# Six stores of a start value issued ahead of the first gather, in a mixer and mixture-of-experts block

## The reference, cut to what matters

```python
logits = (h @ router_w + router_b).astype(jnp.float32)
top_v, top_i = lax.top_k(logits, TOP_K)
gates = jax.nn.softmax(top_v, axis=-1).astype(h.dtype)
...
def expert_block(args):
    xblk, e = args
    gu = xblk @ w_gu[e] + b_gu[e]
    gate = jnp.minimum(gu[:, ::2], SWIGLU_LIMIT)
    up = jnp.clip(gu[:, 1::2], -SWIGLU_LIMIT, SWIGLU_LIMIT)
    act = (up + 1.0) * gate * jax.nn.sigmoid(SWIGLU_ALPHA * gate)
    return act @ w_down[e] + b_down[e]

yb = lax.map(expert_block, (xb, block_e))
y = yb.reshape(-1, D)[dest] * gate_sorted[:, None]
return jnp.zeros_like(h).at[tok_sorted].add(y)
```

## Time and profile before

| | |
|---|---|
| median of 3 runs | 2887.31 us (2883.24 to 2889.01) |
| profiled execution, its own time | 2882.61 us |
| its span in the trace | 2880.8 us |
| PE busy | 2584.2 us, 90% |
| DVE busy | 1755.5 us, 61% |
| ACT busy | 1550.8 us, 54% |
| POOL busy | 761.7 us, 26% |
| moved by q1 (SP and others) | 481.80 MB |
| moved by q0 (POOL) | 47.79 MB |

### The profile page before, as it was taken

The page is one execution under the profiler, slowest core; times in us unless marked ns, Lnnn a source line. Parts: engine busy times, 40 slices in busy tenths (PEclk is TensorE's granted clock), DMA queues, the critical chain, the costliest instruction groups (busy, mean ns, idle before and its releaser), DMA issues. The chain is left out here.

```text
span 2880.8 us, 132861 instructions
## 1 busy us (share of the span) xinstructions
PE 2584.2 (90%) x55873; PEld 2238.8 (78%) x55873; DVE 1755.5 (61%) x1936; ACT 1550.8 (54%) x1833; POOL 761.7 (26%) x586
## 2 busy tenths in 40 slices
PE   8999997898898886699999999998889999999993
PEld 2444556788888754598998998988888999999993
DVE  2344894544545477517264638577787767878883
ACT  3522543433333543517264647577777767768773
POOL 1201003543544212112222222232222322233221
PEclk9999998999999997799999999999999999999997
DMA  9500001000000222818365659698899887979975
GB/s 366 192 30 32 1 1 37 19 26 15 18 25 15 84 96 104 341 24 285 119 209 192 227 173 342 219 329 319 316 351 308 307 291 272 326 276 350 348 276 194
DMA packets 124477, 536.74 MB, mean 186 GB/s; under 512 B 12541, under 2 KB 13553, under 8 KB 91617
## 3 DMA queue, kind: packets, MB, share of 16 engines
q1 hardware_dynamic: 107120, 481.80, 44.6%
q0 software_dynamic: 14464, 47.79, 7.3%
q10 hardware_dynamic: 2832, 6.37, 0.6%
HBM read 496.99 MB, written 38.92 MB: 186 GB/s over the span
## 5 line engine op out<-in xcount | busy, mean ns | idle before, releaser
L2192 PE MATMUL ps<-qkv,weights 128*128 128x64 f16 x10496 | 939.7, 193 | 71.7 <-DVE weights L1686 37.4
L2192 PEld LDWEIGHTS ps<-qkv,weights 128*128 128x128 f16 x10496 | 922.2, 98 | 87.6 <-DVE weights L1686 43.9
L2193 PE MATMUL ps<-qkv,weights 128*128 128x64 f16 x10496 | 939.1, 193 | 2.3 <-issue 2.3
L2194 PE MATMUL ps<-qkv,weights 128*128 128x64 f16 x10496 | 939.1, 193 | 0.0
L2193 PEld LDWEIGHTS ps<-qkv,weights 128*128 128x128 f16 x10496 | 922.9, 98 | 2.4 <-issue 2.4
L2194 PEld LDWEIGHTS ps<-qkv,weights 128*128 128x128 f16 x10496 | 922.9, 98 | 0.0
L1686 DVE SCALAR_TENSOR_TENSOR weights<-hT,weights 128x2048 f16<-128x2048 f32 x256 | 592.5, 2373 | 170.3 <-ACT weights L1147 145.2
L1147 ACT ACTIVATE weights<-hT 128x2048 f16<-128x2048 f32 x256 | 523.2, 2098 | 75.1 <-DMA hT<-in_w_gu_dram 66.2
L2209 PE MATMUL ps<-qkv,weights 128*128 128x64 f16 x5248 | 472.0, 193 | 20.8 <-DVE weights L1691 18.6
L2209 PEld LDWEIGHTS ps<-qkv,weights 128*128 128x128 f16 x5248 | 461.4, 98 | 27.4 <-DVE weights L1691 23.0
L2210 PE MATMUL ps<-qkv,weights 128*128 128x64 f16 x5248 | 471.7, 193 | 0.0
(11 more groups left out here) (395 smaller groups left out, 3979.8 us busy)
## 6 DMA issues: line engine op xcount, KB each, us to landing
hT<-in_w_gu_dram SPq DMA_DIRECT2D x256, 1024.0 KB, 6.9
qkv<-in_w_down_dram SPq DMA_DIRECT2D x128, 1024.0 KB, 5.7
weights<-in_w_ada_dram SPq DMA_DIRECT2D x12, 2048.0 KB, 16.4
qkv<-in_w_in_dram SPq DMA_DIRECT2D x4, 2048.0 KB, 7.7
hT<-decay_rows SPq DMA_DIRECT2D x20, 256.0 KB, 3.3
hT<-beta_rows SPq DMA_DIRECT2D x20, 256.0 KB, 3.9
qkv<-in_x_dram ACTq DMA_DIRECT2D x8, 512.0 KB, 6.6
weights<-in_w_in_dram SPq DMA_DIRECT2D x2, 2048.0 KB, 14.5
```

What stands on the lines that cost most here:

```text
L2192: pe.matmul(dst, ghi[k][:, b, c], xT[:, 0, k, :], start=first, stop=False, skip_group_check=True)
L2193: pe.matmul(dst, ghi[k][:, b, c], xT[:, 1, k, :], start=False, stop=False, skip_group_check=True)
L2194: last = pe.matmul(dst, glo[k][:, b, c], xT[:, 0, k, :], start=False, stop=end, skip_group_check=True)
```

## The change

POOL issues the stores of pieces 0 to 5 ahead of `gather(0)`, and those of pieces 6 and 7 behind it. Nothing is added or taken away; the same transfers are issued by the same engine on the same queue in another order. Pieces 6 and 7 stay behind, since PE makes them only after it has turned the gathered rows.

```diff
             pool.sem_inc(s_al, 1)
+            for n in range(6):
+                store_y_start(n)
             gather(0)
-            for n in range(NT):
+            for n in range(6, NT):
                 store_y_start(n)
             gather(1)
             gather(2)
```

## The result

The changed kernel takes 2895.47 us against 2885.64 us of the kernel before, medians of 20 runs each. The ratio is 1.0032, with a 95% interval of 1.0023 to 1.0041: slower by 9.2 us, between 6.6 and 11.8. The forecast was 2886, in a range up to 2893, with most of the chance on no change.

What follows compares the result with a forecast made beforehand. PE, busy 90% of the span, bounds the kernel, so only its loop's start can move: block 1's turning from 1199.65 to 1198.5 gains 1.1 us, 2882.61 to 2881.5 profiled, 2886.2 on the median. Range 2880 to 2893.

Steps and rivals of the forecast that it cites:

- The queue ahead of the gather: POOL's queue q0: six stores, 3.15 MB, lie ahead of block 0's gather, which lands 8.5 us later, at 1178.7.
- D: How much later block 0's gather lands than before: 8.5 us, with bounds of -0.6 and 14.3.
- Start of the data: On q0, data begins some 1.6 us after an issue's end, so the stores' data starts at 1156.2.
- The transfer: 3.41 MB pass on q0 beside SP's weights, at 0.136 or 0.191 MB a us, until 1175.5.
- From the last byte to landing: Block 0's gather on q0 lands 3.2 us after its last byte, at 1178.7.
- The trap that the prediction named: Skill's "DVE blocks DMA": POOL can't write descriptors while DVE holds their shared port pair; stores 2 to 4 held some 2 us.
- the two bounds of my working for block 0's end: Block 0's matmuls on PE end at 1195.5, set by the last low half, or at 1200.4, shifted as a whole.
- their middle: Block 1's turning on PE was put at 1198.5, between 1196.7 and 1200.4, against 1199.65: a gain of 1.1 us.
- the whole shift: Upper bound for block 0's matmuls on PE: their end moves by all of D, from 1191.9 to 1200.4.
- The slower one: POOL's queue slower than reckoned, at 0.136 MB a us or less, D 14.3 or more: 2893 to 2896, chance 0.18.
- the even trade: Forecast case at the start of the loop: D between 4 and 14, time 2882 to 2892, chance 0.63.
- The rival that the gather doesn't queue: On POOL's queue the gather lands 3.8 to 8.5 us after issue, D up to 4.1: 2880, chance 0.19.

Runs made afterwards that it cites:

- the hold: Kernel before, but SP starts the next expert's five w_gu chunks (5.2 MB) only when PE has turned block 1: ratio 0.9967, 9.5 us faster.
- the wait alone: Kernel before, but POOL waits for piece 5's copy ahead of the first gather, with no store ahead of it: ratio 1.0009, 2.6 us slower.
- stores on SP's queue: Kernel before, but SP issues all eight stores on its own queue and POOL's queue holds gathers alone: ratio 0.9988; with next weights held until block 1's turning, 0.9980.
- five_ahead: Changed kernel, but only stores 0 to 4 go ahead of the first gather and 5 to 7 behind it: ratio 1.0018 to the kernel before, 5.2 us slower.
- five twice: Changed kernel with stores 0 to 4 issued a second time ahead of the gather, into an unread tensor: ratio 1.0050 to the kernel before, 14.4 us slower.
- three ahead: Kernel before, but stores 0 to 2 go ahead of the first gather and 3 to 7 behind it: ratio 0.9997.

## Why the prediction was wrong

**Right.** The stretch, and that nothing behind it takes part. The issue times: five stores ahead of the names, the sixth at 4.4, the gather at 5.3 behind them (forecast 4.2 and 5.1). That DVE's first read would be ended by PE and not by a store (3.31 us, PE). That the late issue is the smaller part. Half right is that stores 6 and 7 would land early: store 7 took 10.0 us in place of 19.9, but it landed at 1193.57 + 10.0 - 2.54 = 1201.0 in the clock of before, 3.5 us later than before and not 2.7 earlier.

**The step that failed: "The queue ahead of the gather", the delay D.** I had 8.5 us; it is 23.0 - 9.6 = 13.4. In the clock of before (2.54 us less than in the rows after) its three terms compare so:

- Start of the data. I took 1.6 us from the end of an issue, so 1156.2 (the sum beside it, 1165.9 less 1163.99, gives 1.9). Up to 1162.0 the trace after shows one packet of q0, so the start is at 1162.0 - 2.54 = 1159.5, 3.3 us later. Of these, 1.2 us are POOL's own: it stood idle for 1.52 us (releaser "issue") between its tables and the first store, which left at 1155.2 in the clock of before and not at 1154.0. The other 2.1 are a longer delay. Counted from the start of the first issue it is 1162.0 - 1157.7 = 4.3 us; before, the first gather began at 1161.70 and q0's first packets fell in 1165.3 to 1166.0, which is 3.6 to 4.3 us. That looks like a fixed delay from the start of an issue, but the other runs show none: with SP's queue full, a first gather on POOL's own empty queue had its first data 3.9 us (before), 4.5 (the hold) and 6.6 us (the wait alone, and both kernels with the stores on SP's queue) after its issue began. What sets it stays open.
- The transfer. I had 19.3 us, at 3.41 / 19.3 = 0.177 MB a us. The rows after have 3.37 MB in the 22 us to 1184 and the last 0.03 in the next two, about 23.5 us in all. Having started later, the stores ran less of their way beside w_down and more beside w_gu, where q0 gets the smaller share, and the end is a thin tail: 0.18 MB in the last four us.
- From the last byte to landing. I had 3.2 us and the gather landed within 1: 2.5 us in my favour.

3.3 + 4.2 - 2.5 = 5.0, which is 13.4 - 8.5 within rounding.

**What I read into 2.29 us.** I took the first gather's long instruction as a sign that DVE's f16 product holds POOL up, and asked whether it would hold the stores too. DVE's product in the kernel after, and then, from the loop of the kernel before, a later gather and the DVE instruction beside it:

```profile
1158.21 2.29 DVE L1655 TENSOR_TENSOR weights<-weights,gdec 128x2048 f16<-128x2048 f16 x1
...
1333.42 2.15 POOL L803 DMA_INDIRECT qkv<-h_scratch,idx  x1 [2.96 <-PE ps L2180]
...
1332.42 2.29 DVE L1686 SCALAR_TENSOR_TENSOR weights<-hT,weights 128x2048 f16<-128x2048 f32 x1 [3.26 <-ACT weights L1147]
```

The product runs over the stores (1157.70 to 1160.51) from the second on, and they take 2.81 us, 0.56 each, as ever: it doesn't hold them. The gather it does hold. The later gather of these rows ends 0.86 us after the end of DVE's instruction (1334.71), as the first one of before ended 1.03 after the product, while gathers beside which DVE is idle take 0.95 to 0.99 in all. In the kernel before, 40 of 84 gathers take over 1.2 us. In the kernel after, the first takes 2.29 at 1168.57 beside a low half of DVE's, which also has two inputs. So it isn't the first gather that is long but any gather issued well inside such an instruction. The Trainium skill (SBUF — State Buffer, "Who interferes with whom") has both halves: a DVE instruction with two SBUF inputs contends with a GpSimd instruction that reads SBUF, not with one that only writes it. The gather reads its row numbers (`idx`) there, and the traces agree. The trap that the prediction named from that page is stated for DVE's 2-port modes, which the page doesn't give to a product of two tensors, and no row here shows a store held. It had no part in the sum.

**What followed from it was right in kind, and luck had a hand in it.** With D = 13.4, the two bounds of my working for block 0's end become 1200.4 and 1205.3, their middle 1202.9; DVE's first read, which PE's end releases, was at 1205.45 - 2.54 = 1202.9. But the middle stood for nothing. The lower bound had only 48 matmuls left when the last low half was done, and in fact PE still had 113 to do behind its stop. The end lies 2.6 us under the whole shift for other reasons: 0.9 us of waiting that went away ahead of the stop, 0.2 in it, and 1.5 of TensorE's clock, which I hadn't forecast. Then the turning of block 1 waited another 0.98 us for its gather, which took 11.7 us to land, so that the queue came last and not PE. From there I carried the branch at 4.4 us. It took 4.9, and another stop of 2.0 us came inside the turning: together 2.5 us that I had listed only as what could make the prediction fail. So block 1's first matmul moved by 6.7 us where the turning that leads to it began only 43.0 - 39.0 = 4.1 late.

**The rivals.** The slower one named the right place, POOL's queue, and its price of 2893 to 2896 holds the 2895.5. I gave it 0.18. Its own conditions weren't met, though: D was 13.4 and not 14.3 or more, q0 had 0.153 MB a us over the 22 us and not 0.136, and block 1's turning began at 1203.7 in the clock of before and not behind 1205.4. By D the run lies at the upper end of the even trade. The two stops at the branch made up what D was short, so that its price came true is partly luck. The rival that the gather doesn't queue is refuted by the 17.6 us of the gather's landing in after and in five_ahead; it allowed 3.8 to 8.5. The range was too narrow: it held D up to 14.3 in the text and yet stopped at 2893, without room for the stops that the text itself named.

**Not settled.** The ratio gives 9.2 us and the two profiled executions 6.8 in the stretch; the lower edge of the interval is 6.6, so they don't contradict each other, but whether a typical execution loses more than the profiled one stays open. What PE's stops are is argued and not shown (see the last section), and why the branch takes 3.3 us on quiet queues was not tried. Nor was it tried what sets the delay to a queue's first data.

## What to carry to other kernels

A small transfer that an engine waits for must not be queued behind large ones that nobody waits for yet, even if the engine that issues them is idle: most of the price isn't the issue but the bytes ahead, divided by the share that the other queues leave. Here it was 9.1 us for 2.6 MB, and 13.4 for 3.1 MB and a late issue. Issue by the time at which the data are needed, across all queues: the largest gain was not in the order on POOL but in keeping 5.2 MB of weights for later off the engines while the start of the loop was filled. And when such a wait is taken away, look at what an "issue" wait (one for which the profile shows no cause) does behind it before booking the gain; of 7.0 us won at one turning, 4.5 were gone by the same block's first matmul.

## What the runs showed of the hardware that was not expected

- Stops of PE without a releaser. A branch of PE over a long body, 68 ns in the median, took 3.3 to 3.9 us with the hold and 4.4 to 6.2 without it, and stops of 1.1 to 2.6 us appeared in the middle of groups of transposes in five kernels without it (after, five ahead, five twice, three ahead, stores on SP's queue). I read them as waits for PE's code. That is an inference: the stop in block 0's matmuls comes at the same place of the program, with 113 left, and the one in the transposes always behind the 13th of 16; and queue q8, which the profile calls "instruction", moves one packet of 0.02 MB just ahead of each stop or during it (before at 1184.0 to 1184.5 and 1201.5 to 1202.0, after at 1199.5 to 1200.0, 1206.0 to 1206.5 and 1211.0 to 1211.5).
- A gather held by DVE. POOL's gather, issued well inside a DVE instruction of 2.29 us with two inputs, ends some 0.9 to 1.1 us after that instruction does and takes up to 2.6 us (2.56 for the first one of the kernel with the wait alone); five stores beside such an instruction took 0.56 us each.
- The start of a queue. While SP's queue was full, POOL's first data came 3.9 to 6.6 us after the start of the first issue (4.3 in the kernel after). On idle queues they came about 1 us after it (store 6 of the kernel after, issued at 1189.65) to 1.5 (the gather at 1202.67 before). A gather on empty queues landed 3.8 to 3.9 us after its issue. Block 0's was turned 5.5 us after its issue behind six stores once SP's queue was quiet, 8.5 in before with SP's queue full, and 10.4 in the kernel with the wait alone, nothing being ahead of it in its own queue in the last two. The Trainium skill (DMA: Bandwidth & Descriptors, "Latency and other measured facts") puts the first byte of POOL's path at about 1 us. The traces agree where the queues are idle; beside a full queue they have four to six times that.
- The share. POOL's queue had 0.136 MB a us beside w_gu (packets of some 8 KB against its own of 4 KB), 0.191 beside w_down (4 KB packets), and 0.41 alone. In company the two queues moved nearly the same number of packets: 377 and 385 beside w_gu, 242 and 239 beside w_down. So the queue with the larger packets got the larger share.
